# Turned-square exchanges through DRAM: writes and reads as separate steps, value products one chunk later, branch C written in two parts

## The reference, cut to what matters

```python
h    = rmsnorm(x, norm_g)
proj = h @ w_in                                   # 2048 x 18512, cut into the sections below
y_a  = spatial_gating(a_u, a_v, a_ws, a_b) * silu(a_z)          # u * (tril(W_s) v + b)
y_b  = (b_bg * conv3_causal(b_cg * b_x)) * silu(b_z)            # depthwise, three taps
y_c  = dsa_attention(c_q, c_k, c_v, i_q, i_k, i_w, rel_bias, 64) * silu(c_z)
m    = sigmoid(g_a) * (y_a @ p_a) + sigmoid(g_b) * (y_b @ p_b) + sigmoid(g_c) * (y_c @ p_c)
out  = rmsnorm(x + m @ w_o, final_g)
```

## Time and profile before

| what | us |
|---|---|
| median of 3 runs (lowest to highest) | 1074.3 (1074.06 to 1075.41) |
| the profiled execution, its own time | 1075.64 |
| its span, first to last instruction | 1073.9 |
| TensorE busy in it | 1053.3 |
| VectorE busy | 625.6 |
| ScalarE busy | 485.1 |
| GpSimd busy | 163.2 |

### The profile page before, as it was taken

The page is one execution under the profiler, slowest core; times in us unless marked ns, Lnnn a source line. Parts: engine busy times, 40 slices in busy tenths (PEclk is TensorE's granted clock), DMA queues, the critical chain, the costliest instruction groups (busy, mean ns, idle before and its releaser), DMA issues.

```text
span 1073.9 us, 14093 instructions
## 1 busy us (share of the span) xinstructions
PE 1053.3 (98%) x4744; PEld 867.4 (81%) x4744; DVE 625.6 (58%) x779; ACT 485.1 (45%) x561; POOL 163.2 (15%) x247
## 2 busy tenths in 40 slices
PE   9999999999999999999999999899999999999997
PEld 7888878888788888878788878688888888888886
DVE  5644555555576555556566675465666566666555
ACT  7444444444454444444344543344445545444443
POOL 1100111111103200222232232213111000000003
PEclk9999999999999999999999999899999999999999
DMA  8776666666666666777677777677877555566553
GB/s 286 210 217 191 197 206 192 190 200 189 189 192 194 195 193 179 236 210 213 190 220 226 218 220 223 210 205 221 239 207 233 196 194 187 184 225 226 196 195 137
DMA packets 113174, 221.01 MB, mean 206 GB/s; under 512 B 11428, under 2 KB 11984, under 8 KB 112752
## 3 DMA queue, kind: packets, MB, share of 16 engines
q1 hardware_dynamic: 104528, 200.43, 61.3%
q0 software_dynamic: 8432, 19.56, 6.5%
q10 hardware_dynamic: 176, 0.53, 0.1%
HBM read 209.46 MB, written 11.02 MB: 205 GB/s over the span
## 4 chain that ended last, share of the span: by engine, by line
PE 89%; DMA 5%; DVE 2%; POOL 1%; ACT 1%; issue 1%; SPq 0%; DVEq 0%; ACTq 0%
PE psum L1093 28%; PE psum L1095 28%; PE psum L1094 28%; DMA keep<-prob_away 2%; DMA prob_away<-keep 1%; PE psum L1102 1%; DMA cg_away<-early 1%; DVE wl L714 1%; DMA yc_away<-early 1%; ACT wh L469 1%; POOL prob_away L372 1%; POOL yc_away L385 1%; DMA keep<-x 0%; PE psum L1240 0%; PE psum L1197 0%
## 5 line engine op out<-in xcount | busy, mean ns | idle before, releaser
L714 DVE TENSOR_TENSOR wl<-raw,wh 128x1024 fp32r<-128x1024 f32 x370 | 455.0, 1231 | 413.5 <-ACT wh L469 413.0
L469 ACT CAST wh<-raw 128x1024 fp32r<-128x1024 f32 x370 | 388.8, 1051 | 557.3 <-PE psum L1095 549.8
L1093 PE MATMUL psum<-wh,hh 128*128 128x512 f32 x1268 | 500.2, 395 | 5.4 <-DVE keep L723 5.4
L1095 PE MATMUL psum<-wh,hl 128*128 128x512 f32 x1268 | 494.9, 390 | 0.0
L1094 PE MATMUL psum<-wl,hh 128*128 128x512 f32 x1268 | 494.8, 390 | 0.0
L1093 PEld LDWEIGHTS psum<-wh,hh 128*128 128x128 f32 x1268 | 239.0, 188 | 58.9 <-DVE keep L723 7.2
L1095 PEld LDWEIGHTS psum<-wh,hl 128*128 128x128 f32 x1268 | 238.7, 188 | 50.4
L1094 PEld LDWEIGHTS psum<-wl,hh 128*128 128x128 f32 x1268 | 239.0, 188 | 49.2
L1093 PE MATMUL psum<-wh,yh 128*128 128x512 f32 x192 | 75.0, 390 | 0.0
L1095 PE MATMUL psum<-wh,yl 128*128 128x512 f32 x192 | 74.7, 389 | 0.0
L1094 PE MATMUL psum<-wl,yh 128*128 128x512 f32 x192 | 74.7, 389 | 0.0
(11 more groups left out here) (173 smaller groups left out, 463.3 us busy)
## 6 DMA issues: line engine op xcount, KB each, us to landing
raw<-w_in SPq DMA_DIRECT2D x288, 512.0 KB, 3.7
raw<-w_o SPq DMA_DIRECT2D x32, 512.0 KB, 3.6
raw<-p_c SPq DMA_DIRECT2D x16, 512.0 KB, 3.6
raw<-p_a SPq DMA_DIRECT2D x16, 512.0 KB, 4.2
raw<-p_b SPq DMA_DIRECT2D x16, 512.0 KB, 4.1
qk_away<-keep POOLq DMA_DIRECT2D x32, 64.0 KB, 3.4
keep<-qk_away POOLq DMA_DIRECT2D x8, 256.0 KB, 3.3
cg_away<-early POOLq DMA_DIRECT2D x32, 64.0 KB, 3.6
```

Source lines behind the costliest of these rows:

```text
L469: act.copy(wh[:, slot, 0:width], raw[:, slot, 0:width]).then_inc(high_split, 1)
L714: dve.tensor_tensor(wl[:, slot, 0:width], raw[:, slot, 0:width], wh[:, slot, 0:width].bitcast(F32), ALU.subtract).then_inc(low_split, 1)
L1093: pe.matmul(dst[t], h, w_h[:, j], start=start, stop=False)
L1095: mm = pe.matmul(dst[t], l, w_h[:, j], start=False, stop=stop)
```

## The change

The semaphore `spilled` becomes one for each kind of exchange. `exchange` is cut into `spill` (four writes) and `fetch` (one read), `exchange_branch` into `spill_branch` (the four writes of one token tile) and `fetch_branch` (two reads), and the waits between them stand where they are called. The reads of the probabilities move on POOL behind the writes of the next head's q and k; PE's `values` and DVE's `gated` move from chunk v+2 to chunk v+3 (so attention work reaches mixing chunk 2). Branch C is written in two parts, in mixing chunks 3 and 4, and read in chunk 6; branch A's blocks are turned into the columns of V instead of those of BZ, and no longer wait for branch C.

```diff
-            def exchange(dst, src, away, landed, free=None):
+            def spill(src, away, spilled):
 
                 count = src.shape[1] // P
                 for i in range(QUARTERS):
                     pool.dma_start(bass.AP(away.tensor, i * TURN, [[P, TURN], [TURN * P, count * QUARTERS], [1, TURN]]),
                                    src[i * TURN:(i + 1) * TURN].rearrange("a (j b) -> a j b", b=TURN)).then_inc(spilled, 16)
-                spills[0] += 16 * QUARTERS
-                pool.wait_ge(spilled, spills[0])
-                if free is not None:
-                    pool.wait_ge(*free)
+
+            def fetch(dst, away, landed):
+
+                count = dst.shape[1] // P
                 pool.dma_start(blk(dst), bass.AP(away.tensor, 0, [[P, P], [P * P, count], [1, P]])).then_inc(landed, 16)
...
+            def fetch_probs(v):
+
+                pool.wait_ge(prob_spilled, 64 * v + 64)
+                if v >= 1:
+                    pool.wait_ge(pv_done, v)
+                fetch(prob_x, prob_away, prob_landed)
+
+            def spill_probs(v):
+
+                pool.wait_ge(prob_turned, v + 1)
+                spill(prob_b, prob_away, prob_spilled)
+
+            for v in range(HEADS):
                 pool.wait_ge(qk_turned, 2 * v + 2)
-                exchange(qk_x, qk_b, qk_away, qk_landed, free=(logit_done, v) if v else None)
...
+                spill(qk_b, qk_away, qk_spilled)
+                if v >= 2:
+                    fetch_probs(v - 2)
+                pool.wait_ge(qk_spilled, 64 * v + 64)
+                if v >= 1:
+                    pool.wait_ge(logit_done, v)
+                fetch(qk_x, qk_away, qk_landed)
+                if v >= 1:
+                    spill_probs(v - 1)
...
+            for c in range(KW):
                 pool.wait_ge(cg_turned, 2 * c + 2)
...
+                spill(cg_b, cg_away, cg_spilled)
+                if c < 2:
+                    fetch_probs(HEADS - 2 + c)
+                pool.wait_ge(cg_spilled, 64 * c + 64)
+                if c >= 1:
+                    pool.wait_ge(conv_step, 4 * c)
+                fetch(cg_x, cg_away, cg_landed)
                 if c == 0:
-                    prob_exchange(HEADS - 1)
-                if c == 1:
+                    spill_probs(HEADS - 1)
+                if c in (3, 4):
                     pool.wait_ge(yc_turned, HEADS)
-                    exchange_branch(section(keep, CZ), section(early, BZ), yc_away, yc_landed)
+                    spill_branch(section(early, BZ), yc_away, yc_spilled, c - 3)
                 if c == 5:
-                    ya_exchange(0)
-            ya_exchange(1)
+                    exchange_ya(0)
+                if c == 6:
+                    pool.wait_ge(yc_spilled, 128)
+                    fetch_branch(section(keep, CZ), yc_away, yc_landed)
+            exchange_ya(1)
...
-                if g == 6 and 2 <= i < 10:
-                    gated(v - 2, i - 2)
+                if g == 6 and 3 <= i < 11:
+                    gated(v - 3, i - 3)
...
-                if c == 0:
-                    dve.wait_ge(yc_landed, 16 * T)
-                dve.transpose(block(early, BZ, c), block(keep, AU, c)).then_inc(ya_turned, 1)
+                dve.transpose(block(early, V, c), block(keep, AU, c)).then_inc(ya_turned, 1)
...
-                if 2 <= i < 10:
-                    values(v - 2, i - 2)
+                if 3 <= i < 11:
+                    values(v - 3, i - 3)
```

More of the change, by code:

```diff
@@ L373, in exchange, with spill_branch, fetch_branch @@
                                    src[i * TURN:(i + 1) * TURN].rearrange("a (j b) -> a j b", b=TURN)).then_inc(spilled, 16)
-                spills[0] += 16 * QUARTERS
-                pool.wait_ge(spilled, spills[0])
-                if free is not None:
-                    pool.wait_ge(*free)
+            def fetch(dst, away, landed):
+                count = dst.shape[1] // P
                 pool.dma_start(blk(dst), bass.AP(away.tensor, 0, [[P, P], [P * P, count], [1, P]])).then_inc(landed, 16)
-            def exchange_branch(dst, src, away, landed):
+            def spill_branch(src, away, spilled, t):
                 count = src.shape[2] // P
[L383 to L388, removed]
+                for i in range(QUARTERS):
+                    pool.dma_start(bass.AP(away.tensor, t * KW * P * P + i * TURN, [[P, TURN], [TURN * P, count * QUARTERS], [1, TURN]]),
+                                   src[i * TURN:(i + 1) * TURN, t].rearrange("a (j b) -> a j b", b=TURN)).then_inc(spilled, 16)
+            def fetch_branch(dst, away, landed):
+                count = dst.shape[2] // P
                 for t in range(T):
@@ L393, in _ @@
                 pool.wait_ge(iq_turned, c + 1)
-                exchange(iq_x, iq_b, iq_away, iq_landed, free=(index_done, c) if c else None)
+                spill(iq_b, iq_away, iq_spilled)
+                pool.wait_ge(iq_spilled, 64 * c + 64)
+                if c >= 1:
+                    pool.wait_ge(index_done, c)
+                fetch(iq_x, iq_away, iq_landed)
             pool.wait_ge(score_step, 1 + 4 * HEADS)
@@ new lines, in exchange_ya @@
+            def exchange_ya(h):
+                src = early[:, :, (V + h) * N:(V + h + 1) * N]
+                pool.wait_ge(ya_turned, 4 * h + 4)
+                for t in range(T):
+                    spill_branch(src, ya_away, ya_spilled, t)
+                pool.wait_ge(ya_spilled, 128 * h + 128)
+                fetch_branch(keep[:, :, (AU + h) * N:(AU + h + 1) * N], ya_away, ya_landed)
+            for c in range(KW):
+                pool.wait_ge(cg_turned, 2 * c + 2)
+                spill(cg_b, cg_away, cg_spilled)
+                if c < 2:
+                    fetch_probs(HEADS - 2 + c)
+                pool.wait_ge(cg_spilled, 64 * c + 64)
+                if c >= 1:
+                    pool.wait_ge(conv_step, 4 * c)
+                fetch(cg_x, cg_away, cg_landed)
@@ L1263, in mixing_chunk @@
                     if g == 1:
-                        if i < 2:
+                        if i < 3:
                             attention(8 + c, 8 + c)
```

12 lines of the change are left out of this document (3 added, 9 removed).

## The result

| kernel | median us | lowest to highest | runs |
|---|---|---|---|
| before | 1074.18 | 1073.02 to 1075.41 | 4 |
| changed | 1059.99 | 1059.26 to 1060.22 | 4 |

The ratio is 0.9867, with a 95% interval of 0.9849 to 0.9884: 14.2 us faster. The profiled execution of the changed kernel took 1060.22 us with a span of 1058.5, against 1075.64 and 1073.9: 15.4 us, the sum of the prediction, worked out against that same execution of the kernel before.

What follows compares the result with a forecast made beforehand. TensorE's waits and slow stretches bound the kernel; 6.5 + 1.65 + 7.5 - 0.23 = 15.4 us takes the profiled 1075.64 to 1060.2, and the median forecast, adjusted for the 1.34 difference, is 1059.3 us, range 1057.9 to 1062.5.

Steps and rivals of the forecast that it cites:

- The bound: Whole kernel: TensorE busy 1053.3 of 1073.9 us, so only its standstills and slow running can be won.
- The probabilities: Value products waiting for probabilities to be read back: all four waits go with values one chunk later, 6.5 us.
- The slow stretch: Attention chunk from 522.65 to 547.40, half clock behind a wait: gone with the wait, 1.65 us, possibly zero in other executions.
- Branch C: Mixing chunk 2: conv factors no longer held up on POOL by branch C's exchange, so the conv read lands in time, 7.5 us.
- The added 0.23: Mixing chunk 2: DVE has gated(7) ahead of the conv, charged as a 0.23 us loss.
- POOL's new wait: POOL's fetch_probs waits for the earlier values; hidden under the landing of the q and k writes, costs nothing.
- Branch C in chunks 3, 4 and 6: Branch C's writes and reads in their new places: cost nothing, with up to 1 us kept for the range.
- The wait in mixing chunk 0: Rival: head 6's probabilities read lands behind the conv writes and delays VectorE there, 0.5 to 2.5 us, 1059.8 to 1061.8; 15%.
- A late conv in chunk 2: Rival: chunk 2's conv still late, or branch C's parts delay chunk 3 or 4; part of 7.5 returns, 1063 at half; 8%.
- values waiting in the new place: Rival: values still wait one chunk later, so 6.5 and 1.65 us stay, 1067.4; 2%.
- the slower case: Rival: probabilities land after VectorE wants to turn the next head's, in each of eight heads; 1076.5 or more, 2%.
- The term that was off: Profiled execution to median, 1.34 us: profiling offset gives 1058.9, a missing slow stretch 1060.5; 1059.3 chosen.

Runs made afterwards that it cites:

- the two kernels that keep the waits: Kernel before with only branch C's exchange changed, 1066.97 us; kernel before with branch C's writes in place but its reads behind chunk 2's conv exchange, 1066.14 us.
- the one-go kernel: Changed kernel with the probabilities written, waited for and read in one go, values still one chunk later: 1059.98 us.
- The 1072.8 us above: Slowest, profiled execution of the kernel before with branch C's writes in place and its reads behind chunk 2's conv exchange; median 1066.14 us.
- first experiment: Changed kernel with branch C's exchange in one go behind the conv read of mixing chunk 2, values still one chunk later: 1066.17 us.

## Why the prediction was right, point by point

**The bound** was read rightly: only TensorE's waits and its slow stretches could be won. **The probabilities**, 6.5 us: the four waits are gone and the intervals are 23.1. **The slow stretch**, 1.65 us: no interval with one is left, and it came again in the two kernels that keep the waits, behind a 2.9 us wait in one, and 3.0 and 2.0 in the other. That it belongs to the waits is so shown; that not every wait has one is shown too. The prediction left open that it is absent from the runs of before. At least 15 of the 27 with a recorded clock, those at 0.991 or 0.993, have as much half clock as the profiled execution, which had this stretch and the one at 690. **Branch C**, 7.5 us: from mixing matmul to mixing matmul it fell from 29.77 to 22.46, and putting branch C ahead of another chunk's conv moved the stall there. **The added 0.23**: 22.46 against 22.24, and gating two sub-blocks earlier takes it away. **POOL's new wait**: 0.75 us, covered; even 8.4 us of it in the one-go kernel cost nothing. **Branch C in chunks 3, 4 and 6**: nothing, and in one piece at chunk 3 nothing either.

**The rivals.** The wait in mixing chunk 0 did not come. The read of head 6's probabilities went out at 614.46 behind the conv writes, and VectorE had no idle time before its turning or the conv; timeline of VectorE, changed kernel:

```profile
623.11 0.58 DVE L891 STREAM_TRANSPOSE keep<-keep 128x384 f32<-128x384 f32 x1
...
625.53 0.42 DVE L949 TENSOR_SCALAR early<-early,conv_t 128x256 f32<-128x256 f32 x1
```

The conv's writes had landed at 619.19, 4.7 us behind their issue (611.89 + 2.58 = 614.47), with the read in flight beside them. That is as in the kernel before (4.6) and not the 7.3 that the rival took from a place with 1 MB of branch reads beside them. The read itself, from the list of DMAs issued between 611 and 616:

```profile
keep<-prob_away POOLq DMA_DIRECT2D x1, 192.0 KB, 5.0
```

It landed 5.0 us after 614.46, at 619.5, 0.3 behind the conv's writes. The same holds for all seven of these reads from 495 us on: they landed 0.1 to 1.7 us behind the writes issued ahead of them, with a median of 4.3 us from issue to landing over the kernel, against 3.6 before. The Trainium skill (DMA: Bandwidth & Descriptors, "Two DMAs through the same engine are not ordered") has descriptors of one queue start in order, and these rows agree, as far as landings can tell of starts. The prediction had no row for this, saying that a read and a write of POOL's are never in flight together before. They are once: branch C's second read, issued between 670.15 and 671.93, took 7.4 us, and the conv's writes went out from 671.92 with it in flight. But the read of the probabilities was not a whole 5.1 us later than the writes, as the rival priced it; it ran beside them, and had 3.6 us of room before L891. A late conv in chunk 2, values waiting in the new place, and the slower case are all absent.

**The term that was off** is the one that turned the profile's time into a median. I took the 1.34 us between the profiled execution of before (1075.64) and the median of its runs for an offset of profiling or for a missing slow stretch, held the offset for likelier, and came to 1059.3 between 1058.9 and 1060.5. No run shows such an offset: in the changed kernel the profiled execution, 1060.22, is one of the four runs and lies 0.2 from their median, and with gating at g = 4 it is the fastest of five. The 1.34 is the kernel before's own spread, which is 10 us wide over 31 runs, and much of its source is what the change removes. The sum for the profiled execution, 1060.2, was the right forecast of the median too, and for a reason: a profile's time less that execution's own stalls comes to the same, whichever execution it was. The 1072.8 us above less 8.4 of idle time, 5 x 0.27 and 3.2 for its two slow stretches gives 1059.9. That the recorded 1059.3 lies only 0.7 below the measured 1059.99 is in part luck: the 0.9 us taken off the sum had no cause in the kernel, and it was small. The gain itself depends on which runs of before one meets: 14.2 us in the first set, 17.1 in the third (1077.09 to 1060.03, ratio 0.9843, 0.982 to 0.9867) and 16.2 in the fourth (1076.37 to 1060.14).

## What to carry to other kernels

A wait of 0.3 to 3 us at the end of a long chain of small steps comes or stays away from pass to pass. Move the consumer by a little more than the largest lateness seen, and the mean falls by the waits and the spread with them. Two sub-blocks did it here where eight were taken. On a queue that runs in order, the expensive thing is not an exchange but the wait in its middle when something with a due time stands behind it: put write and read apart, or start the whole exchange where the next timed item is farthest away. A stall costs more than its idle time, here about 0.27 us for each and up to 2.1 more for a slow clock, so measure from start to start of something that comes once per pass.

## What the runs showed of the hardware

Half clock behind a stall does not follow from the length of the idle time alone. Idle times of 1.74 (first experiment, at 8.23), 1.84 (before, at 521.66), 1.99, 2.88, 2.95, 4.17 and 5.2 us had a stretch at 0.50, the 1.2 GHz level, at their end or within 1.2 us of it; in the longest it began 2.4 us before TensorE went on. Those of 1.83 (before, at 473.33), 2.45, 1.43 and 1.41 and all shorter ones had none. Each stretch between the chunks cost 1.4 to 2.1 us by the intervals. The Trainium skill (TensorE: Matmul & The Clock Gate, "What's actually happening") has the number of slow matmuls at a kernel's start vary between runs of one kernel. No row here counts those at the start; what varies here is the mean granted clock of a whole run, from 0.991 to 0.996 over 27 runs of before. So what a stall costs is its idle time, a restart and, at some of the stalls, up to 2.1 us more.
